# Ten expert steps written out, with a third staging set for the weights of chunks 4, 7 and 10

## What is computed

```python
dense_w = jnp.sum(jax.nn.one_hot(eid, N_EXPERTS) * tw[..., None], axis=-2)   # two of 16 experts a token
hid = jnp.einsum('bsd,edf->bsef', h, lp['moe_w1'])        # 1024 -> 2 x 256
gate, up = jnp.split(hid, 2, axis=-1)
act = jax.nn.silu(gate) * up * dense_w[..., None]
return jnp.einsum('bsef,efd->bsd', act, lp['moe_w2'])     # 256 -> 1024
```

## Time and profile before

| what | us |
|---|---|
| three runs | 1814.97, 1817.40, 1821.79; median 1817.4 |
| profiled execution | 1818.29 |
| its span | 1816.2, with 2.1 around it |

### The profile page before, as it was taken

The page is one execution under the profiler, slowest core; times in us unless marked ns, Lnnn a source line. Parts: engine busy times, 40 slices in busy tenths (PEclk is TensorE's granted clock), DMA queues, the critical chain, the costliest instruction groups (busy, mean ns, idle before and its releaser), DMA issues.

```text
span 1816.2 us, 34273 instructions
## 1 busy us (share of the span) xinstructions
PE 1649.1 (91%) x13317; PEld 1112.9 (61%) x13317; DVE 1171.0 (64%) x1877; ACT 891.5 (49%) x1477; POOL 491.3 (27%) x434
## 2 busy tenths in 40 slices
PE   5899989999989996988889999899999999799886
PEld 3478766777765555444466886667776655554444
DVE  4495355777636757888556926477774394788874
ACT  3322555666642232777543236466664312358763
POOL 0222253221231311233143315322113321123313
PEclk8999999999999998999979999999999999889998
DMA  9565535532335645999935542232223366489975
GB/s 318 185 210 176 170 133 186 195 112 73 100 122 211 208 142 211 339 378 401 323 146 167 195 160 93 80 103 73 77 77 106 125 235 233 151 299 338 402 291 197
DMA packets 191615, 351.33 MB, mean 193 GB/s; under 512 B 15795, under 2 KB 99314, under 8 KB 191218
## 3 DMA queue, kind: packets, MB, share of 16 engines
q1 hardware_dynamic: 182005, 320.17, 50.2%
q0 software_dynamic: 7776, 28.32, 4.2%
q10 hardware_dynamic: 1693, 0.89, 0.2%
HBM read 288.32 MB, written 61.01 MB: 192 GB/s over the span
## 4 chain that ended last, share of the span: by engine, by line
PE 65%; DVE 11%; DMA 9%; ACT 7%; issue 5%; DVEq 2%; SPq 1%; POOL 1%; ACTq 0%; POOLq 0%
PE PS L444 38%; PE PS L451 11%; PE PS L1179 3%; DMA wf<-in_moe_w 3%; PE PS L1163 3%; DMA arena<-in_moe_w 3%; PE PS L949 2%; DVE arena L2560 2%; PE PS L914 1%; ACT whi L1760 1%; PE PS L931 1%; ACT arena L1591 1%; DMA hpart<-y_rows,wulo 1%; DVE wlo L2560 1%; DVE scratch L2500 1%
## 5 line engine op out<-in xcount | busy, mean ns | idle before, releaser
L1883 POOL TENSOR_TENSOR wlo<-wf,whi 128x256 f16<-128x256 f32 (+1 forms) x276 | 294.8, 1101 | 851.2 <-ACT whi L1507 799.3
L444 PE MATMUL PS<-hpart,whi 128*128 128x320 f16 x2048 | 423.4, 300 | 19.0 <-ACT arena L1591 17.8
L444 PE MATMUL PS<-hpart,wlo 128*128 128x320 f16 x1024 | 306.6, 299 | 0.0
L444 PE MATMUL PS<-whi,hpart 128*128 128x256 f16 (+2 forms) x1536 | 287.8, 288 | 9.9 <-issue 6.3
L444 PEld LDWEIGHTS PS<-hpart,whi 128*128 128x128 f16 x2048 | 190.1, 98 | 108.7 <-issue 39.7
L444 PE MATMUL PS<-wlo,hpart 128*128 128x256 f16 (+2 forms) x768 | 219.5, 288 | 0.0
L444 PEld LDWEIGHTS PS<-whi,hpart 128*128 128x128 f16 x1536 | 148.7, 98 | 66.9 <-issue 29.6
L2366 DVE TENSOR_REDUCE stat<-PS 128x1 f32<-128x640 f32 (+1 forms) x160 | 110.7, 713 | 80.0 <-PE PS L1163 77.5
L451 PE MATMUL PS<-hpart,whi 128*128 128x128 f16 (+1 forms) x768 | 138.8, 304 | 12.4 <-DVE hpart L2041 10.8
L1591 ACT ACTIVATE arena<-PS,pcol 128x320 f32<-128x320 f32 x128 | 67.4, 527 | 168.2 <-PE PS L444 163.1
L2194 DVE SCALAR_TENSOR_TENSOR scratch<-scratch,cw 128x655 f32<-128x655 f32 x120 | 138.6, 1197 | 4.5
(11 more groups left out here) (366 smaller groups left out, 2909.2 us busy)
## 6 DMA issues: line engine op xcount, KB each, us to landing
arena<-in_moe_w SPq DMA_DIRECT2D x68, 1024.0 KB, 8.9
arena<-in_w_ada SPq DMA_DIRECT2D x48, 1024.0 KB, 7.1
wf<-in_w_gate SPq DMA_DIRECT2D x32, 1024.0 KB, 5.7
wf<-in_moe_w SPq DMA_DIRECT2D x32, 1024.0 KB, 8.9
g_rows<-arena SPq DMA_DIRECT2D x128, 160.0 KB, 1.8
wf<-in_w_in SPq DMA_DIRECT2D x18, 1024.0 KB, 9.4
y_rows<-scratch SPq DMA_DIRECT2D x34, 512.0 KB, 8.7
arena<-g_rows SPq DMA_DIRECT2D x24, 640.0 KB, 5.2
```

What stands on the lines that cost most here:

```text
L444: ins = pe.matmul(out, st, mv, start=first and n == 0, stop=last and n == 2)
L1883: ins = pool.tensor_tensor(lo[:, a:b], wf[j][:, a:b], hi[:, a:b], ALU.subtract)
```

## The change

- Chunks 4, 7 and 10 are staged in the third set; the others up to 10 alternate between sets 0 and 1, and from chunk 11 on it is two sets again (staged). A load of chunks 5 to 12 waits for the chunk three back.
- Ten steps (chunks 0 to 9 on ACT, DVE and SP, 0 to 10 on PE, gathers 3 to 12 on POOL) are written out, and the loop does the rest.
- SP issues chunk 4's loads and parts 1 and 2 of chunk 3 right behind its wait for the first gather, and only then the 19 small loads.
- PE turns the rows of chunk 1 ahead of chunk 0's products, into banks of their own, and begins chunk 1's products ahead of turning chunk 0's activations.
- The early list holds the first 16 chunks instead of 3. The whole list (places, list_whole, listed) is made in steps 6 to 8 in a place of its own, the columns of the weights in step 8. DVE multiplies before it makes the low half of the rows.

```diff
 rowhot = scratch[:, 0:640].bitcast(F16).rearrange("p (n q) -> p n q", n=10)
-chhot = scratch[:, 640:640 + 5 * (CHUNKS + 2)].bitcast(F16).rearrange("p (n c) -> p n c", n=10)
+rowall = arena[:, 20480:21120].bitcast(F16).rearrange("p (n q) -> p n q", n=10)
...
+third_in = [Signal(x_in[0].sem, 4 * 16, 16), Signal(x_in[1].sem, 4 * 16, 16), sig("third_in", 3 * 16)]
 xg_in = [sig(f"xg_in{j}") for j in range(2)]
...
 def staged(c):
-    return (0, 1, 0, 1, 2)[c] if c < 5 else 1 - c % 2
+    return (0, 1, 0, 1, 2, 0, 1, 2, 0, 1, 2)[c] if c < 11 else 1 - c % 2
 def arrivals(c):
-    return (1, 1, 2, 2, 1)[c] if c < 5 else (c + 1) // 2
+    return (1, 1, 2, 2, 1, 3, 3, 2, 4, 4, 3)[c] if c < 11 else (c - 1) // 2
+def rows_in_psum(c):
+    return PS[:, 3 if isinstance(c, int) and c == 1 else 0, :].rearrange("p (k n) -> p k n", k=KC)
...
-                         ).then_inc((m_once if j == 2 else m_in[3 * j + q]).sem, 16)
+                         ).then_inc((third_in[q] if j == 2 else m_in[3 * j + q]).sem, 16)
...
-            before = {3: 1, 5: 2, 6: 3}.get(c, c - 2)
+            before = 1 if c == 3 else c - 3
...
         for tile in range(TILES):
             sp.wait_ge(*rows_whole(l, tile + 1))
             sp.dma_start(t["h2_rows"][P * tile:P * tile + P, :], htok[:, tile, :]).then_inc(rows_out.sem, 16)
+        sp.wait_ge(*first_in(l, 16))
+        for q in range(3):
+            load_early(4, q)
+        for q in range(1, 3):
+            load_early(3, q)
         if ahead:
             rows_load(sp, l + 1)
             params_load(sp, l + 1)
-        sp.wait_ge(*first_in(l, 16))
-        for q in range(1, 3):
-            load_early(3, q)
-        for q in range(3):
-            load_early(4, q)
         load_early(5, 0)
         sp.wait_ge(started.sem, 1)
         sp.wait_ge(*route_ready(l, 1))
...
                 sp.wait_ge(mw_lo2.sem, past + (c - 1))
             load(ds(e, 1), j, q)
-        load_early(5, 1)
-        load_early(6, 0)
         sp.wait_ge(*filled(0, CHUNKS * 16))
         def store(c, j, row):
...
+        for c in range(10):
+            if c < 8:
+                load_early(c + 5, 1)
+                if c:
+                    load_early(c + 4, 2)
+            elif c == 8:
+                load_early(12, 2)
+            else:
+                load_next(13, 1, 0, 13)
             store(c, c % 2, P * c)
-            for part in parts:
-                load_early(*part)
-        with sp.Fori(3, p + 1) as i:
+            if c < 7:
+                load_early(c + 6, 0)
+            elif c > 7:
+                load_next(c + 5, 0, c % 2, c + 5)
+        with sp.Fori(5, p) as i:
             for n in range(2):
-                store(i * 2 + (n - 2), n, i * (2 * P) + (n - 2) * P)
-                load_next(i * 2 + (2 + n), 1, 1 - n, i * 2 + (2 + n))
-                load_next(i * 2 + (2 + n), 2, 1 - n, i * 2 + (2 + n))
-                load_next(i * 2 + (3 + n), 0, n, i * 2 + (3 + n))
+                load_next(i * 2 + (4 + n), 1, 1 - n, i * 2 + (4 + n))
+                load_next(i * 2 + (3 + n), 2, n, i * 2 + (3 + n))
+                store(i * 2 + n, n, i * (2 * P) + n * P)
+                load_next(i * 2 + (5 + n), 0, n, i * 2 + (5 + n))
+        load_next(p * 2 + 4, 1, 1, p * 2 + 4)
+        load_next(p * 2 + 3, 2, 0, p * 2 + 3)
         store(p * 2, 0, p * (2 * P))
-        load_next(p * 2 + 4, 1, 1, p * 2 + 4)
         load_next(p * 2 + 4, 2, 1, p * 2 + 4)
         store(p * 2 + 1, 1, p * (2 * P) + P)
...
             for n in range(10):
-                ins = pe.matmul(bank(5)[:, 0:CHUNKS + 2], rowhot[:, n, :], chhot[:, n, :], start=n == 0,
+                ins = pe.matmul(bank(5)[:, 256:256 + CHUNKS + 2], rowall[:, n, :], chhot[:, n, :], start=n == 0,
                                 stop=n == 9)
             ins.then_inc(list_all.sem, 1)
...
+        def turn_rows(c, j, ci, first=False, pair=0):
             if first:
                 pe.wait_ge(*first_in(l, 16))
             else:
                 pe.wait_ge(xg_in[j].sem, ran * 16 + ci * 16)
-                pe.wait_ge(hs_ready.sem, past + c)
+                if pair == 0:
+                    pe.wait_ge(hs_ready.sem, past + c)
             rows = xg0 if first else xg[j]
             for k in range(KC):
-                ins = pe.transpose(PS[:, 0, k * P:(k + 1) * P], rows[:, k * P:(k + 1) * P], ident[:, :])
+                ins = pe.transpose(PS[:, pair, k * P:(k + 1) * P], rows[:, k * P:(k + 1) * P], ident[:, :])
             ins.then_inc(ht_done.sem, 1)
...
-        busy(10)
+        busy(6)
         turn_rows(0, 0, 0, True)
-        busy(3)
-        gate_up(0, 0, range(3), True)
-        turn_rows(1, 1, 1)
-        gate_up(0, 0, range(3, KC))
+        turn_rows(1, 1, 1, pair=3)
+        gate_up(0, 0, range(KC), True)
+        gate_up(1, 1, range(3))
         turn_act(0, 0, True)
-        list_whole()
+        gate_up(1, 1, range(3, 5))
+        turn_rows(2, 0, 1)
+        gate_up(1, 1, range(5, KC))
+        down(0, 0)
+        turn_act(1, 1)
+        for c in range(2, 11):
+            gate_up(c, c % 2, range(5))
+            turn_rows(c + 1, 1 - c % 2, c // 2 + 1)
+            gate_up(c, c % 2, range(5, KC))
+            down(c - 1, 1 - c % 2)
+            if c == 8:
+                list_whole()
+            turn_act(c, c % 2)
         pe.wait_ge(started.sem, 1)
         pe.wait_ge(*route_ready(l, 1))
         p = pairs_now(pe)
-        with pe.Fori(0, p + 1) as i:
+        with pe.Fori(5, p + 1) as i:
             for n in range(2):
...
             if slot == 2:
-                act.wait_ge(*m_once(l, 3 * 16))
+                act.wait_ge(*third_in[q](l, count * 16))
             else:
-                act.wait_ge(m_in[3 * slot + q].sem, ran * 16 + count * 16)
+                act.wait_ge(m_in[3 * slot + q].sem, ran * 16 + (count * 16 - 16 * l))
             if not isinstance(c, int) or c >= 2:
                 act.wait_ge((my_done if q == 2 else mgu_done).sem, past + c)
...
-            act.copy(hshi[j], PS[:, 0, :].rearrange("p (k n) -> p k n", k=KC)).then_inc(hs_hi.sem, 1)
+            act.copy(hshi[j], rows_in_psum(c)).then_inc(hs_hi.sem, 1)
...
         part_early(2, 0)
-        for c in range(4):
+        for c in range(10):
...
+        for c in range(3, 13):
+            pool.wait_ge(ht_done.sem, past + (c - 1))
+            pool.tensor_tensor(zero1[:, :], zero1[:, :], zero1[:, :], ALU.add)
+            pool.drain()
+            rows_from(xg[c % 2], idxall[:, c:c + 1], xg_in[c % 2])
         pool.wait_ge(*idx_all(l, 1))
         pool.wait_ge(started.sem, 1)
         pool.wait_ge(*route_ready(l, 1))
         p = pairs_now(pool)
-        with pool.Fori(0, p + 1) as i:
+        with pool.Fori(5, p + 1) as i:
             for n in range(2):
                 pool.wait_ge(ht_done.sem, past + (i * 2 + (2 + n)))
...
+            dve.tensor_copy(idxall[:, EXPERTS:], bank(5)[:, 256 + EXPERTS:256 + CHUNKS + 2]).then_inc(idx_all.sem, 1)
+        def gate_columns():
...
         loops()
...
+        rows_low(1, 1)
         dve.wait_ge(mw_lo.sem, past * 2 + 3)
         part_low(1, 1, 1, 5)
         part_low(1, 1, 2, 6)
-        rows_low(1, 1)
...
         part_low(0, 0, 0, 7)
-        listed()
-        dve.wait_ge(*rexp_ready(l, 1))
-        dve.tensor_reduce(rcol[:, 3, :], ex5[:, :, 0:4], AX_X, ALU.add)
-        dve.tensor_scalar(rcol[:, 4, :], ex5[:, :, 4], 1.0, None, ALU.add)
-        dve.drain()
-        dve.tensor_tensor(rcol[:, 5, :], rcol[:, 3, :], rcol[:, 4, :], ALU.mult)
-        dve.drain()
-        dve.reciprocal(rcol[:, 3, :], rcol[:, 5, :])
...
+            multiply(c + 1, 1 - c % 2)
             rows_low(c + 2, c % 2)
-            multiply(c + 1, 1 - c % 2)
             part_low(1 - c % 2, staged(c + 3), 0, 3 * c + 9)
+            if c == 6:
+                places()
+            if c == 8:
+                gate_columns()
         dve.wait_ge(started.sem, 1)
         dve.wait_ge(*route_ready(l, 1))
         p = pairs_now(dve)
-        with dve.Fori(2, p + 1) as i:
+        with dve.Fori(5, p + 1) as i:
             for n in range(2):
                 c, j = i * 2 + (1 + n), 1 - n
                 act_low(i * 2 + n, n)
                 part_low(n, 1 - n, 1, i * 6 + (7 + 3 * n))
                 part_low(j, n, 2, i * 6 + (8 + 3 * n))
```

More of the change, by code:

```diff
@@ L318, in build @@
         w_lo = sig("w_lo", V_ALL, 1)
-        x_in = [sig(f"x_in{n}", 16) for n in range(2)]
+        x_in = [sig(f"x_in{n}", 4 * 16) for n in range(2)]
         x_hi, x_lo = sig("x_hi", 2), sig("x_lo", 2)
@@ L1296, in list_whole @@
                     for n in range(10):
-                        ins = pe.matmul(bank(5)[:, 0:CHUNKS + 2], rowhot[:, n, :], chhot[:, n, :], start=n == 0,
+                        ins = pe.matmul(bank(5)[:, 256:256 + CHUNKS + 2], rowall[:, n, :], chhot[:, n, :], start=n == 0,
                                         stop=n == 9)
                     ins.then_inc(list_all.sem, 1)
-                def turn_rows(c, j, ci, first=False):
```

(47 more changed lines are left out.)

21 lines of the change are left out of this document (10 added, 11 removed).

## The result

| kernel | median us | runs |
|---|---|---|
| before | 1816.18 | 4 |
| changed | 1786.47 (1785.22 to 1791.57) | 4 |

The ratio is 0.9828, with a 95% interval of 0.9804 to 0.9851: 1.7% faster. The prediction was 1796, with a range of 1785 to 1808, so time and sign were right. That the time still fell into the range is in part luck.

The account below looks back on a forecast made before the run. The prediction took the transfers to bound the end of each expert stage. Holes of 13.6 and 14.1 us, less 4 and 1, gave 22.7 us off 1818.3, so 1795.6, stated as 1796, range 1785 to 1808.

Parts of the forecast that it names:

- The bytes bound the end: Expert stages of both layers: the end comes when the bytes are in, sooner only if transfers waste less before 780 and 1662.
- What the holes are worth: Both expert stages: against 399 and 402 GB/s, 13.6 us are wasted in the first layer and 14.1 in the second.
- The third set: Middle stretches, 740 to 780 and 1634 to 1662 us: loads issued a step sooner keep transfers full, worth 16.1 us by bytes.
- The front: Start of each stage: chunk 4's loads right after the first gather fill the holes at 716 and 1598 us.
- The charge of 4 us for the small loads: First layer's front: 19 small loads now delay chunk 5, leaving a hole charged 4 us; their former place cost nothing.
- The engines' gain is cover and not a term: PE, ACT and DVE: earlier start and 8.9 us steps could save 24 and 23 us, more than transfers permit, so not counted.
- The added wait for the second gather: PE before chunk 0's products: free if the gather lands by 715; at worst 1 to 2 us late, covered by the lead.
- The queue does not run dry when two sets return: SP's loads: queue grows to seven or eight by step 6, loses 0.4 in each of steps 7 to 9, never empties.
- Stores queue behind weights: Rival, steps 5 to 8: stores land in 19.7 us, ACT held 2 us a step; 1812 if the lead is smaller; chance 0.06.
- Slower by code: Rival, ten written-out steps: instructions must be fetched while queues are full; at 4 us a step, 1852 us; chance 0.06.
- The sum: Both layers: 9.6 us in the first and 13.1 in the second, 22.7 together, giving 1795.6, stated as 1796.

Follow-up runs that it names:

- half_stores: The changed kernel storing only 64 of the 128 result rows of each chunk; ratio 0.9774 to the kernel before, stages 157.1 and 157.6 us.
- front_old: The changed kernel with SP's order at the front as before the change, all else kept; ratio 0.9875 to the kernel before, stages 168.0 and 165.8 us.
- small_late: The changed kernel with the 19 small loads moved behind the stores of chunks 2 and 3; ratio 0.9812 to the kernel before, stages 162.6 and 159.7 us.
- multiply_old: The changed kernel with DVE making the low half of the rows before it multiplies; ratio 0.9804 to the kernel before, stages 164.4 and 159.7 us.
- small_first: The changed kernel with the 19 small loads back ahead of the wait for the first gather; ratio 0.9821 to the kernel before, stages 164.0 and 160.5 us.
- list_old: The changed kernel with the list's work and the weights' columns back between chunks 0 and 1; ratio 0.9843 to the kernel before, stages 164.2 and 161.8 us.
- old_order_two: The changed kernel with two staging sets and SP's old order in the steps; ratio 0.9974 to the kernel before, stages 180.1 and 176.5 us.
- sp_alone: The kernel before with only SP's queue changed, new step order and new front; ratio 0.9893 to the kernel before, stages 168.3 and 170.1 us.
- two_sets: The changed kernel with two staging sets from chunk 5 on, all else kept; ratio 0.9824 to the kernel before, stages 164.4 and 161.4 us.

## Why the prediction was right or wrong

- **The bytes bound the end: right.** half_stores and front_old show it, with 8.4 and 9 us expected of them and 7.1 and 9.8 measured where bytes bind. The second layer is bound by the engines as well, within 2 us.
- **What the holes are worth: nearly right.** The changed kernel runs at 403 to 406 GB/s where 399 and 402 were put; that is 1 to 2 us a layer.
- **The third set: this step failed.** It was to bring 16.1 of 22.7 us and is worth 1.8 in this change. The prediction took from the number of sets that loads could not be issued sooner, and did not ask what SP was waiting for when a place was already free. In the kernel before a free place stood open for 5 to 6 us in the middle while SP waited for another. The new order of SP's queue removes that wait, and with it two sets make 404 and 396 GB/s there; undoing it costs 30.8 us with two sets and 15.6 with three. By itself, in the kernel before, it brings the stretch from 310 and 299 to 346 and 362 only: the front and the engines' start do the rest. The new order stood in the diff, but the prediction followed SP's queue through the front only. Set and order overlap, so neither has a price of its own, and under the old order the third set is worth 17.0 us, near the 16.1 that the prediction gave it.
- **The front: direction right, first layer mis-sized.** Net 0.7 us was forecast in the first and 5.9 in the second; front_old gives 3.8 and 6.0. The charge of 4 us for the small loads was too high: 1.5 us by small_late. And they had slowed the first gather by 2 us, which the prediction gave out as costing nothing.
- **The engines' gain is cover and not a term: wrong for the start, right for the steps.** multiply_old costs nothing. The start on PE costs 12.6 us of stages when undone alone, since it sets when splits are made, and so when loads are issued; where the bytes come in all the same, as in small_first and list_old, chunk 1's late SiLU costs the first stage nothing. Chunk 1's SiLU came 20.0 us after the gather's issue, instead of 28.7 before. The steps came out at 9.07 on average where 8.9 was put. DVE's order, to which the prediction gave the whole 1.1 us of the longer ones, is 0.2 of it (9.47 against 9.28); what took them from 10.0 to 9.47 no run shows.
- **The added wait for the second gather: right.** PE had it at 712.41, and chunk 0's products ran from 713.34.
- **The queue does not run dry when two sets return: right,** 406 GB/s from 780 to 850.
- **Stores queue behind weights: the mechanism came, its cover held.** From 740 to 850 us a store took 14.1 us to land (8.7 in the earlier trace rows), loads 14.7 to 17.6 and gathers 8.3. ACT waited for stores, as the waits of the changed kernel from 760 to 820 us say, us in total, times, longest:

```profile
ACT scratch L1833 <- DMA y_rows<-scratch: 14.0, 6, 2.6
```

  2.3 us in each of six steps, against 2 forecast. It cost nothing, because the bytes were late by more: the transfers made 403 to 406 GB/s in that time. Loads and stores of SP's queue took 5 to 8 us longer to land, the gathers on POOL's did not; this agrees with what the prediction cites of the Trainium skill, "DMA: Bandwidth & Descriptors", Queues, rings and completion order, on the ring order of SP's queue.
- **Slower by code: did not come.** PE's longest idle time for want of issue is 1.7 us as before.
- **The sum.** It was 8.6 us short: 5 in the first stage, 2 in the second, 1.4 outside. For the 5 the sooner gather (2), the smaller hole (2.5) and the rate (1 to 2) are at hand; how they share it is not shown. The sum came near although its largest part had the wrong cause, because the holes were counted in bytes: their size did not depend on what filled them. It was luck that the change held another thing, the order, that filled them.
- **Open.** Under the old order the late stretch makes 363 GB/s in old_order_two and 399 in the kernel before, at the same number of sets; why faster engines make it worse was not tried. The profile shows a granted clock of 0.90 there. And sp_alone's 12.7 us to two_sets are assigned only as above.

## What to carry to other kernels

Where one queue issues loads that each wait for a place to come free, list the moments at which the places come free and compare them with the order of the queue; a permutation may do what a further buffer was meant to. When transfers bound a stage, count the bytes that its holes lack: every filled hole counts, wherever it lies, and an engine's late start counts if it frees a place. Measure a change of several parts in pairs, because two remedies for the same wait hide each other.

## What was not expected of the hardware

The queue's depth moved the time to land of SP's own transfers only: gathers from POOL took 8.8 us while SP's loads landed after 9.0, and 8.3 while these took 14.7 to 17.6. Nineteen small loads of under 0.9 MB in all slowed a gather of 0.5 MB beside them from 4.5 to 5.9 us in front_old, and to 6.5 in small_first and the kernel before.
